# Where the steps of the adaLN product stand: eight of them from RG-LRU to the first FFN, all sixteen in pairs

## The chip, the cores and the metric

One NeuronCore of a Trainium2 chip runs the whole model as one program, written with explicit semaphores. The metric is device time of that core in microseconds. The engines are TensorE (PE), VectorE (DVE), ScalarE (ACT), GpSimd (POOL) and SyncE (SP), whose queue starts nearly all transfers of weights.

## The reference

Two blocks on a sequence of 256 tokens with 1024 features, all in float32. What matters here:

```
# first block: layer 0 = pool and attention mixer, conv FFN; layer 1 = RG-LRU mixer, conv FFN
z = causal_dwconv(h @ w_in, conv_w, conv_b)           # conv FFN, w_in 1024 x 5632
u, g = jnp.split(z, 2, axis=-1);  y = (gelu(g) * u) @ w_out
...
z = h @ w_in;  gate, xr = jnp.split(z, 2, axis=-1)    # RG-LRU, w_in 1024 x 2560
xr = causal_dwconv(xr, conv_w, conv_b)
r = sigmoid(xb @ w_a + b_a);  i = sigmoid(xb @ w_x + b_x)   # 10 blocks of 128
log_a = -8 * r * softplus(-lam);  a = exp(log_a)
b = sqrt(-expm1(2 * log_a)) * (i * xr)
hs = scan(a, b);  y = (gelu(gate) * hs) @ w_out
# second block, adaLN: needs only c, an input
mod = silu(c) @ ada_w + ada_b                          # 1024 by 1024 x 6144
sh1, sc1, gt1, sh2, sc2, gt2 = split(mod, 6)
h = rms_norm(x) * (1 + sc1) + sh1                      # first use of mod
```

## The kernel before

Activations lie transposed, features on partitions: a tile is 128 features by 256 tokens. Weights come in pieces of 128 by 8 tiles of 128 (512 KB) into a ring of nine buffers, `ring`, in the order that `weight_order` writes; piece n goes into buffer n mod 9, and SP starts its transfer once piece n - 9 has been used (`used`). ScalarE copies each piece rounded to the matmul's format (`whi`, seven buffers) and VectorE makes the rest (`wlo`); both do so in `feed`, which runs ahead of the piece at hand by a fixed number of positions in that order (ACT up to 6, DVE up to 5). A column of output, 128 features, is then 24 matmuls on TensorE: eight times whi by hh, whi by hl and wlo by hh.

The product `silu(c) @ ada_w` is cut in 24 steps (`mod_step`). A step takes two pieces of `ada_w`, which take positions in the ring but need no whi and wlo, and on TensorE four matmuls in the source (eight in the trace), each 32 columns of the array by 512. Eight steps make one part (a third of `mod`). A part's eighth step is followed by a copy to `mrow` on ScalarE, and later by `mod_turn`, which transposes the part and adds `ada_b`. The part's PSUM bank is held from its first step to that copy. The first part is made in the attention mixer. `ADA_RG` puts the second in RG-LRU: behind x columns 5, 7 and 9 and behind gate columns 1, 3, 5, 7 and 9. `ADA_IN` puts the third in the second FFN's input, behind columns 2, 5, 8, 11, 14, 17, 19 and 21. In that input a "column" m is one column of u and one of g.

RG-LRU goes like this. TensorE makes x columns 0 to 9 (0 to 2 together, with `early`), and between them the gate products `ri` for blocks whose x column is convolved (`RI`: blocks 0 and 1 behind x column 5, 2 behind 6, 3 and 4 behind 7, 5 behind 8, 6 and 7 behind 9, 8 and 9 behind gate column 0). It then makes gate columns 0 to 9 and `rg_w_out`, which takes all eight PSUM banks. VectorE, for each x column, first feeds wlo and then does the convolution (`taps`, three instructions on `xr`); later come `decline` on `rr`, `size` (on `sc` and `xr`), `inputs`, `scan`, `times_gate` and `low_of_y`, which writes `yl`. ScalarE has the sigmoids, `bends` (tanh, `xr<-rr`), `decays` (exp, `rr<-rr`), `roots` and the gelus. `size(0)` is the first that needs `decays(0)`, and `decays(0)` stands behind gate column 1 on ScalarE. The order on every engine is the order of the code.

## Time and profile before

| what | value |
|---|---|
| median of 3 runs | 1094.45 us (1092.57 to 1095.63) |
| profiled execution, its own time | 1092.14 us |
| span in the trace | 1089.8 us |
| TensorE busy | 97% of the span |
| VectorE busy | 76% |
| ScalarE busy | 57% |
| granted TensorE clock, mean | 0.989 of full speed |

The profile is of one execution, by the hardware profiler. Starts are in us from the span's start. A busy share is an average over stages with different limits, so the stages that the change touches are read one by one: the first FFN's input runs from about 126 to 242 us, RG-LRU from about 306 to 401 us, and the second FFN's input from about 413 to 540 us. "Idle before" in a row names who released the engine.

### The profile page before, as it was taken

What the parts mean: (1) busy time and instruction counts of PE and PEld (TensorE: products, weight loads), DVE (VectorE), ACT (ScalarE), POOL (GpSimd) and SP (SyncE); (2) the same over time, 40 slices, a digit from 0 to 9 for tenths busy, and PEclk for the clock granted to TensorE, in tenths of its full rate; (3) what the DMA queues carried; (4) which work ended last, traced back from release to release, by engine and by line L of the source; (5) the groups of instructions that cost most, each with busy time, mean ns of one, the idle gap of its engine ahead of it and who ended that gap; (6) DMA issues with size and microseconds to landing.
All of it is one profiled execution on the core that took longest, in us unless ns stands there. A gap on an engine that the chain in (4) does not pass through costs nothing.

```text
span 1089.8 us, 20955 instructions
## 1 busy us (share of the span) xinstructions
PE 1052.1 (97%) x8608; PEld 998.0 (92%) x8608; DVE 829.6 (76%) x1418; ACT 626.0 (57%) x1056; POOL 72.2 (7%) x79
## 2 busy tenths in 40 slices
PE   8999999999999999999999997999999999999996
PEld 7876999999998799999999897899989989999996
DVE  6466799888887979988788789998955777655452
ACT  7545686666667867665656683122343468875340
POOL 1222200000102010000001000000000030000010
PEclk8999999999999999999999999999999989999998
DMA  9358465566676956677766542232433555566651
GB/s 347 129 188 308 163 212 194 194 180 196 198 251 219 319 171 217 217 253 231 252 203 205 185 131 75 82 98 92 149 111 110 176 189 177 182 190 182 187 155 39
DMA packets 59422, 200.39 MB, mean 184 GB/s; under 512 B 6720, under 2 KB 10432, under 8 KB 59200
## 3 DMA queue, kind: packets, MB, share of 16 engines
q1 hardware_dynamic: 57600, 194.54, 55.1%
q10 hardware_dynamic: 1728, 4.53, 1.2%
q8 instruction: 68, 1.11, 0.4%
q14 instruction: 26, 0.21, 0.1%
HBM read 197.99 MB, written 1.05 MB: 183 GB/s over the span
## 4 chain that ended last, share of the span: by engine, by line
PE 83%; DVE 9%; ACT 5%; DMA 2%; issue 1%; ACTq 0%; SPq 0%; POOL 0%; DVEq 0%
PE ps L481 82%; DVE wlo L1575 2%; ACT whi L1051 1%; ACT L1051 1%; DVE rst L1608 1%; DVE raw L1575 1%; DVE hl L1575 1%; ACT raw L1051 1%; ACT hh L1051 1%; DMA ring<-rg_w_in 1%; DMA ring<-pa_w_in 0%; DMA ring<-w_o 0%; DVE bks L1575 0%; DMA ring<-pa_w_out 0%; PE ps L666 0%
## 5 line engine op out<-in xcount | busy, mean ns | idle before, releaser
L481 PE MATMUL ps<-hh,whi 128*128 128x256 f32 (+1 forms) x1656 | 473.0, 286 | 4.2 <-DVE wlo L1575 3.6
L481 PE MATMUL ps<-hl,whi 128*128 128x256 f32 (+1 forms) x1656 | 462.8, 279 | 0.0
L481 PE MATMUL ps<-hh,wlo 128*128 128x256 f32 (+1 forms) x1656 | 462.6, 279 | 0.0
L1575 DVE TENSOR_TENSOR wlo<-ring,whi 128x1024 fp32r<-128x1024 f32 (+2 forms) x314 | 376.5, 1214 | 53.0 <-ACT whi L1051 52.6
L1051 ACT ACTIVATE whi<-ring 128x1024 fp32r<-128x1024 f32 (+2 forms) x314 | 320.9, 1038 | 57.1 <-PE ps L481 39.7
L481 PEld LDWEIGHTS ps<-hh,whi 128*128 128x128 f32 x1656 | 314.8, 190 | 25.2 <-issue 14.8
L481 PEld LDWEIGHTS ps<-hl,whi 128*128 128x128 f32 x1656 | 313.3, 189 | 1.3 <-issue 1.0
L481 PEld LDWEIGHTS ps<-hh,wlo 128*128 128x128 f32 x1656 | 313.7, 189 | 0.0
L481 PE MATMUL ps<-hidh,whi 128*128 128x256 f32 x608 | 169.3, 278 | 0.0
L481 PE MATMUL ps<-hidl,whi 128*128 128x256 f32 x608 | 169.1, 278 | 0.0
L481 PE MATMUL ps<-hidh,wlo 128*128 128x256 f32 x608 | 169.1, 278 | 0.0
L481 PEld LDWEIGHTS ps<-hidh,whi 128*128 128x128 f32 x608 | 115.2, 190 | 0.8 <-issue 0.8
L481 PEld LDWEIGHTS ps<-hidl,whi 128*128 128x128 f32 x608 | 114.1, 188 | 0.0
L481 PEld LDWEIGHTS ps<-hidh,wlo 128*128 128x128 f32 x608 | 114.1, 188 | 0.0
L2380 POOL TENSOR_TENSOR sqa<-sqa,sqt 128x256 f32<-128x256 f32 x36 | 40.5, 1124 | 890.7 <-ACT sqt L1051 890.7
L1051 ACT ACTIVATE sqt<-x 128x256 f32<-128x256 f32 x49 | 20.1, 414 | 59.2 <-DVE x L1581 35.1
L1581 DVE SCALAR_TENSOR_TENSOR zg<-ps,vec,zg 128x255 f32<-128x255 f32 x84 | 40.4, 481 | 15.1 <-ACT zg L1051 11.6
L1581 DVE SCALAR_TENSOR_TENSOR zu<-ps,vec,zu 128x255 f32<-128x255 f32 x80 | 38.5, 481 | 10.4 <-ACT zu L1051 9.0
L1051 ACT ACTIVATE zg<-ps,vec 128x256 f32<-128x256 f32 x42 | 23.6, 561 | 34.0 <-PE ps L481 34.0
L1051 ACT ACT_TABLE_LOAD x32 | 41.1, 1283 | 3.3 <-PE ps L481 1.6
L481 PE MATMUL ps<-yin,ring 128*128 128x256 f32 x160 | 39.0, 379 | 0.1
L1581 DVE SCALAR_TENSOR_TENSOR x<-ps,mod,x 128x256 f32<-128x256 f32 x16 | 7.6, 483 | 40.6 <-PE ps L481 40.6
(365 smaller groups left out, 1335.3 us busy)
## 6 DMA issues: line engine op xcount, KB each, us to landing
ring<-ffn_w_in SPq DMA_DIRECT2D x88, 512.0 KB, 3.7
ring<-ffn_w SPq DMA_DIRECT2D x64, 512.0 KB, 3.9
ring<-w_in SPq DMA_DIRECT2D x51, 512.0 KB, 3.3
ring<-ada_w SPq DMA_DIRECT2D x48, 512.0 KB, 4.3
ring<-ffn_w_out SPq DMA_DIRECT2D x32, 448.0 KB, 3.4
ring<-rg_w_in SPq DMA_DIRECT2D x20, 512.0 KB, 4.6
ring<-ffn_w_out SPq DMA_DIRECT2D x16, 512.0 KB, 3.6
ring<-pa_w_in SPq DMA_DIRECT2D x15, 512.0 KB, 6.9
```

The source lines that it names most:

```text
L481: return e.matmul(o, l, r, start=start, stop=stop)
L1051: return e.activation(o, i, func, bias=bias, scale=scale, accum_out=acc)
L1575: return e.tensor_tensor(o, a, b, op)
L1581: return e.scalar_tensor_tensor(out=o, in0=a, scalar=s, in1=b, op0=op0, op1=op1)
L1608: e.reciprocal(rst[:, :], rst[:, :]).then_inc(*mean.up(("rst", n)))
L2380: e.tensor_tensor(sqa[:, :], sqa[:, :], sqt[:, m % 2, :], ADD).then_inc(*sum_g.up((n, m)))
```

## The change

The second part's eight steps are made in the first FFN's input and no longer in RG-LRU. In both FFN inputs the eight steps stand in pairs, two behind each of columns 5, 10, 15 and 20. `mod_turn` of the second part moves from the second FFN's input (column 4 on TensorE, 6 on VectorE) to the first FFN's output, where the call in `also` was there already. The number of steps, their matmuls and their transfers stay as they are. The order of the ring's pieces follows.

```
-ADA_IN = ((), (2, 5, 8, 11, 14, 17, 19, 21))
-ADA_RG = ((5, 7, 9), (1, 3, 5, 7, 9))
+ADA_IN = ((5, 5, 10, 10, 15, 15, 20, 20), (5, 5, 10, 10, 15, 15, 20, 20))
...
@@ weight_order, and in the same way conv_ffn of TensorE, VectorE and ScalarE (mod_step) @@
-            if m in ADA_IN[l]:
+            for _ in range(ADA_IN[l].count(m)):
                 columns()
...
                     whole("rg_w_in", 8, (m + 10 - 10 * n,))
-                    if m in ADA_RG[n]:
-                        columns()
...
@@ conv_ffn of TensorE; on VectorE the same with m == 6 @@
-                    if m == 4:
-                        mod_turn()
...
@@ rglru of TensorE, and in the same way of ScalarE and VectorE @@
-                    if m in ADA_RG[0]:
-                        mod_step()
...
-                    if m in ADA_RG[1]:
-                        mod_step()
```

TensorE, first FFN's input, where the g column of column 5 ends and the u column of 6 begins. Before:

```order
L481 MATMUL ps<-hh,whi_8 128x256
L481 MATMUL ps<-hl,whi_8 128x256
L481 MATMUL ps<-hh,wlo_30 128x256
L481 MATMUL ps<-hh,whi_9 128x256
L481 MATMUL ps<-hl,whi_9 128x256
L481 MATMUL ps<-hh,wlo_31 128x256
```

Now the same place reads as follows (`sc` is silu(c), and an adaLN step is two of these rows):

```order
L478 MATMUL ps<-hh,whi_8 128x256
L478 MATMUL ps<-hl,whi_8 128x256
L478 MATMUL ps<-hh,wlo_30 128x256
L478 MATMUL ps<-ring_22,sc_44 32x512 x2
L478 MATMUL ps<-ring_23,sc_44 32x512 x2
L478 MATMUL ps<-ring_15,sc_44 32x512 x2
L478 MATMUL ps<-ring_16,sc_44 32x512 x2
L478 MATMUL ps<-hh,whi_9 128x256
L478 MATMUL ps<-hl,whi_9 128x256
```

Two steps now stand where one column followed the other.

VectorE in RG-LRU, from behind the convolutions of x columns 0 to 2, which read `xl`. Before (`wlo` is a piece's low part; each group of three rows on `xr` is the taps of one column, here 3, 4 and 5):

```order
L1575 TENSOR_TENSOR wlo_32<-ring_23,whi_8 128x1024
L1581 SCALAR_TENSOR_TENSOR xr<-ps,vec,xr 128x255
L1581 SCALAR_TENSOR_TENSOR xr<-ps,vec,xr 128x254
L1581 SCALAR_TENSOR_TENSOR xr<-ps,vec,xr 128x253
L1575 TENSOR_TENSOR wlo_24<-ring_15,whi_9 128x1024
L1581 SCALAR_TENSOR_TENSOR xr<-ps,vec,xr 128x255
L1581 SCALAR_TENSOR_TENSOR xr<-ps,vec,xr 128x254
L1581 SCALAR_TENSOR_TENSOR xr<-ps,vec,xr 128x253
L1581 SCALAR_TENSOR_TENSOR xr<-ps,vec,xr 128x255
L1581 SCALAR_TENSOR_TENSOR xr<-ps,vec,xr 128x254
L1581 SCALAR_TENSOR_TENSOR xr<-ps,vec,xr 128x253
```

Now:

```order
L1562 TENSOR_TENSOR wlo_28<-ring_19,whi_8 128x1024
L1562 TENSOR_TENSOR wlo_29<-ring_20,whi_9 128x1024
L1562 TENSOR_TENSOR wlo_30<-ring_21,whi_10 128x1024
L1568 SCALAR_TENSOR_TENSOR xr<-ps,vec,xr 128x255
L1568 SCALAR_TENSOR_TENSOR xr<-ps,vec,xr 128x254
L1568 SCALAR_TENSOR_TENSOR xr<-ps,vec,xr 128x253
L1562 TENSOR_TENSOR wlo_31<-ring_22,whi_11 128x1024
L1568 SCALAR_TENSOR_TENSOR xr<-ps,vec,xr 128x255
L1568 SCALAR_TENSOR_TENSOR xr<-ps,vec,xr 128x254
L1568 SCALAR_TENSOR_TENSOR xr<-ps,vec,xr 128x253
L1562 TENSOR_TENSOR wlo_32<-ring_23,whi_12 128x1024
```

Three low parts (x columns 6, 7 and 8) stand ahead of the taps of column 3, where one stood, because no ada_w pieces take positions of the ring between them.

ScalarE in RG-LRU, from gate column 1 to `decays` (`gate<-ps` is the gate column, `xr<-rr` tanh, `rr<-rr` exp). Before:

```order
L1051 ACTIVATE gate<-ps 128x256
L1051 ACTIVATE whi_9<-ring_21 128x1024
L1051 ACTIVATE whi_10<-ring_22 128x1024
L1051 ACTIVATE xr<-rr 128x512
L1051 ACT_TABLE_LOAD
L1051 ACTIVATE rr<-rr 128x1024 x2
```

Now, with the last feed ahead of the column:

```order
L1042 ACTIVATE whi_12<-ring_21 128x1024
L1042 ACTIVATE gate<-ps 128x256
L1042 ACTIVATE xr<-rr 128x512
L1042 ACT_TABLE_LOAD
L1042 ACTIVATE rr<-rr 128x1024 x2
```

The two whi copies that stood between the gate column and tanh are gone from there; one stands ahead of the column.

## Rows read from the trace of the kernel before

**Rows 1.** The page, part 1: busy time of each engine.
```profile
PE 1052.1 (97%) x8608; PEld 998.0 (92%) x8608; DVE 829.6 (76%) x1418; ACT 626.0 (57%) x1056; POOL 72.2 (7%) x79
```

**Rows 2.** Who waited for whom, TensorE: total, times, longest.
```profile
PE ps L481 <- ACT mrow L1051: 2.6, 1, 2.6
```

**Rows 3.** Windows: busy us by engine, then TensorE's granted clock.
```profile
150.00:170.00 20.00, 20.00 (x179) 20.00 (x178) 19.68 (x35) 14.13 (x24) 0.00 (x0) 1.00 0.59 188
...
310.00:330.00 20.00, 20.00 (x156) 18.45 (x155) 19.35 (x36) 13.45 (x25) 3.16 (x3) 1.00 0.72 239
330.00:350.00 20.00, 20.00 (x147) 16.17 (x146) 14.14 (x27) 14.38 (x26) 5.34 (x7) 1.00 0.68 214
...
370.00:390.00 20.00, 17.41 (x153) 16.41 (x152) 20.00 (x27) 13.79 (x18) 0.00 (x0) 1.00 0.77 263
```

**Rows 4.** Timeline of TensorE, steps behind gate columns 1 and 3.
```profile
348.59 1.06 PE L481 MATMUL ps<-ring,sc 128*32 128x512 f32 x8
349.58 0.38 PE L481 MATMUL ps<-hh,whi 128*128 128x256 f32 x1
...
355.24 1.07 PE L481 MATMUL ps<-ring,sc 128*32 128x512 f32 x8
```

**Rows 5.** Timeline of TensorE, second half of that first step.
```profile
349.04 0.61 PE L481 MATMUL ps<-ring,sc 128*32 128x512 f32 x4
```

**Rows 6.** TensorE, steps of the second FFN: first pair of rows.
```profile
444.42 1.07 PE L481 MATMUL ps<-ring,sc 128*32 128x512 f32 x8
...
461.95 1.06 PE L481 MATMUL ps<-ring,sc 128*32 128x512 f32 x8
```

**Rows 7.** TensorE, steps of the second FFN: second pair of rows.
```profile
514.53 1.06 PE L481 MATMUL ps<-ring,sc 128*32 128x512 f32 x8
...
526.61 1.07 PE L481 MATMUL ps<-ring,sc 128*32 128x512 f32 x8
```

**Rows 8.** TensorE in RG-LRU: x column 6, then gate products.
```profile
322.39 0.38 PE L481 MATMUL ps<-hh,whi 128*128 128x256 f32 x1
...
328.93 1.89 PE L481 MATMUL ps<-xr,wab 128*128 128x256 f32 x8
```

**Rows 9.** TensorE in RG-LRU: gate products of blocks 8 and 9.
```profile
343.94 1.89 PE L481 MATMUL ps<-xr,wab 128*128 128x256 f32 x8
```

**Rows 10.** VectorE in RG-LRU.
```profile
320.39 1.23 DVE L1575 TENSOR_TENSOR wlo<-ring,whi 128x1024 fp32r<-128x1024 f32 x1
...
339.15 1.52 DVE L1581 SCALAR_TENSOR_TENSOR xr<-ps,vec,xr 128x255 f32<-128x255 f32 x3 [0.25 <-ACT xr L1051]
...
353.90 1.23 DVE L1575 TENSOR_TENSOR sc<-rr 128x1024 f32<-128x1024 f32 x1 [1.48 <-ACT rr L1051]
...
366.07 1.23 DVE L1575 TENSOR_TENSOR wlo<-ring,whi 128x1024 fp32r<-128x1024 f32 x1 [1.05 <-ACT whi L1051]
...
377.06 0.68 DVE L1575 TENSOR_TENSOR yl<-gate,yh 128x512 fp32r<-128x512 f32 x1
```

**Rows 11.** ScalarE in RG-LRU.
```profile
348.70 0.38 ACT L1051 ACTIVATE gate<-ps 128x256 f32<-128x256 f32 x1 [1.04 <-PE ps L481]
348.98 2.00 ACT L1051 ACTIVATE whi<-ring 128x1024 fp32r<-128x1024 f32 x2
350.88 0.62 ACT L1051 ACTIVATE xr<-rr 128x512 f32<-128x512 f32 x1
```

**Rows 12.** TensorE at the start of rg_w_out.
```profile
378.83 0.36 PE L481 MATMUL ps<-yh,whi 128*128 128x256 f32 x1 [2.59 <-ACT mrow L1051]
```

**Rows 13.** Landing times of ada_w pieces.
```profile
DMA to landing us min/median/max: 3.6/4.3/8.2
```

**Rows 14.** TensorE in the mixers behind its longest wait.
```profile
672.63 1.12 PE L481 MATMUL ps<-ws,gvT 128*64 128x128 f32 x16 [3.40 <-ACT gvT L1051]
```

**Rows 15.** Windows behind that wait: busy us, TensorE's granted clock.
```profile
672.00:676.00 4.00, 3.37 (x28) 3.23 (x29) 3.89 (x8) 2.95 (x6) 0.00 (x0) 0.75 0.02 4
676.00:680.00 4.00, 3.94 (x24) 3.37 (x25) 3.83 (x18) 2.66 (x4) 0.00 (x0) 0.82 0.11 33
```

More of the change, by code:

```diff
@@ L709, in conv_ffn @@
                     give((w, m + 22), ff_dve, (l, "g", m))
-                    if m in ADA_IN[l]:
+                    for _ in range(ADA_IN[l].count(m)):
                         mod_step()
-                    if m == 4:
-                        mod_turn()
                 def also(m):
@@ L1272, in conv_ffn @@
                     behind(m)
-                    if m in ADA_IN[l]:
+                    for _ in range(ADA_IN[l].count(m)):
                         mod_step()
@@ L1338, in rglru @@
                         ri(i)
-                    if m in ADA_RG[0]:
-                        mod_step()
                 bends(0)
@@ L1347, in rglru @@
                         act(gate[:, m, :], out_of("rg_w_in", m), ACT.Gelu_apprx_tanh).then_inc(*rg_act.up(("gelu", m)))
-                    if m in ADA_RG[1]:
-                        mod_step()
                     for i in RI[m + 10]:
@@ L1924, in conv_ffn @@
                     behind(m)
-                    if m in ADA_IN[l]:
+                    for _ in range(ADA_IN[l].count(m)):
                         mod_step()
-                    if m == 6:
-                        mod_turn()
                 behind(22)
@@ L2000, in rglru @@
                         decline(i)
-                    if m in ADA_RG[0]:
-                        mod_step()
                 for m in range(10):
@@ L2006, in rglru @@
                         decline(i)
-                    if m in ADA_RG[1] and m < 9:
-                        mod_step()
                     for g in {2: (0, 1), 3: (2,)}.get(m, ()):
@@ L2021, in rglru @@
                         low_of_y(2)
-                        mod_step()
                 for k in range(10):
```

## The prediction

> **What bounds the kernel now.** I read the busy times first. TensorE works for 1052.1 us [rows 1] of a span of 1089.8, so only some 38 us of the span are waits, and a change that moves TensorE's work can win or lose only what waits before or after it. The list of who waited for whom shows where: of the waits in the stages that the change touches only one is of any size, 2.6 us put down to ScalarE's `mrow` copy [rows 2]. It stands at the start of `rg_w_out`, at 378.83 [rows 12]. The windows by stage then say what is behind it. In the first FFN's input TensorE is busy for 20.00 of 20 us while VectorE is at 19.68 (150 to 170). In RG-LRU TensorE is also at 20.00 until 370, with VectorE at 19.35 from 310 to 330 and at 14.14 from 330 to 350; from 370 to 390 TensorE falls to 17.41 and VectorE has 20.00 [rows 3]. So the first FFN's input is bound by TensorE alone, whatever VectorE's load. RG-LRU begins bound by TensorE with VectorE nearly full, and ends on a chain through VectorE. That is the point of the whole forecast: work taken off TensorE in RG-LRU comes back only as far as VectorE and ScalarE get done earlier, while the same work put in the FFN costs its full length.
>
> **What a step costs.** Between the starts of two steps of RG-LRU lie 6.65 us, which hold one step and two columns (348.59 and 355.24) [rows 4]. In the second FFN 17.53 us hold one step and six columns [rows 6] and 12.08 us hold one step and four [rows 7]. The difference of the last two gives a column 5.45 / 2 = 2.725 us, and what is left is 1.18 us for a step there; in RG-LRU it is 6.65 - 5.45 = 1.20. I take 1.20.
>
> **What a second step behind the first costs.** The trace of before has no such pair. A step is eight matmuls, four at a time on four strips of the array. Its first four start at 348.59, its second four at 349.04 [rows 5], and the next column's first matmul at 349.58 [rows 4]. Four thus follow four at 0.45 us, and going back to whole-array matmuls takes 0.54; the rest of the 1.20 is going in and loading weights. A second step should add 2 x 0.45 = 0.90, so a pair costs 2.10 where two single steps cost 2.40. Bounds: no gain, 0, if each step pays its entry again, and 0.30 a pair if not. I take 0.30, because the four second matmuls of a step already follow its first four without a gap for the change of pieces (they read the step's second half).
>
> The Trainium skill, on TensorEngine Tiling (Array Packing), Key Properties, says that changing the tiling mode drains the array; by it a pair pays that once for two steps, and the sum would be the same as mine.
>
> **The sum, part by part.** First FFN's input: eight steps come in, as four pairs, 4 x 2.10 = +8.4. Nothing hides them, since TensorE has no idle time there [rows 3]. Second FFN's input: eight single steps become four pairs, 4 x (2.10 - 2.40) = -1.2. `mod_turn` of the second part (a copy's transposes, in any place on TensorE) only moves from one stage bound by TensorE to another, and I cost it at nothing.
>
> RG-LRU: eight steps go, 9.6 us of TensorE's work. How much earlier does `rg_w_out` start? I follow the chain.
>
> 1. VectorE up to the taps of x column 9. They end at 339.15 + 1.52 = 340.67 [rows 10]. From 320.39 it is nearly full. Without ada_w pieces in the ring its feed runs farther ahead, and nine low parts, not six, stand ahead of those taps. Three more at some 1.15 us end the taps 3.45 us later, less the idle time that they fill. The work from 320.39 counts to 22.6 us at the pace of its own rows (9 low parts at 1.15, 7 taps at 1.52, 1.6 of `decline`), so the taps end between 343.0 and 343.9 us. I take 343.4.
> 2. TensorE wants those taps for the gate products of block 9. Without steps it starts x column 6 when its low part is made, 320.39 + 1.15 = 321.55, where it started at 322.39 [rows 8, 10]. From there to the products of blocks 3 and 4 are 6.54 us (322.39 to 328.93) [rows 8], and from those to block 8's product 15.01 us (to 343.94) [rows 9], of which 2.40 were the steps behind x columns 7 and 9. Block 8's product now starts at about 321.55 + 6.54 + 12.61 = 340.7, and block 9's could at 341.65. It waits until 343.4. From products of both blocks to the end of gate column 1 were 343.94 to 348.59 [rows 4, 9], 4.65; less 0.95 for block 8 that is 3.7. Gate column 1 ends at 347.1, 1.5 earlier than before, not the 3.6 of the three steps that went.
> 3. ScalarE. Behind gate column 1 it made two high parts for 1.90 us (348.98 to 350.88), then tanh, a table load and exp, and VectorE began `size` at 353.90 [rows 10, 11]. Now both high parts are gone from there. `size` starts 1.5 + 1.9 = 3.4 earlier, at 350.5.
> 4. VectorE from `size` to the first `yl`: 353.90 to 377.06 + 0.68 = 377.74, of which it idled 1.05 [rows 10]. The chain has six low parts before and after, so its work is the same 22.8 us, and the low parts' high parts are ready earlier. That is 1.05 more, and the first `yl` is done at 373.3.
> 5. `rg_w_out` began 1.09 behind that `yl`, since it takes all eight banks and one was freed only by `mrow` [rows 2, 12]. No part is held in RG-LRU now: 1.0 more.
>
> Together 1.5 + 1.9 + 1.05 + 1.0 = 5.5 us earlier. TensorE itself would be there at 347.1 + 8 x 2.725 = 368.9, so it waits 4.4 us where it waited 2.59: what is late next is `yl`. Bounds of the 5.5: 9.6 if TensorE alone decided (plus the old wait of 2.59 at most); below, 4.0, if point 1 costs all that the three steps gave and only points 3 to 5 stay.
>
> Sum: 8.4 - 1.2 - 5.5 = +1.7 us. On the profiled execution that is 1092.14 + 1.7 = 1093.8. The median of the runs lies 2.3 above that execution, so for a median I say 1096.1.
>
> **The rivals.** (a) RG-LRU gives everything back. For it speaks that VectorE had 5.9 idle us from 330 to 350 [rows 3]; against it that the idle time stands behind the stretch where it is full. Then the sum is 8.4 - 1.2 - 9.6 = -2.4, and with the old wait gone too -5.0. Chance 0.12.
>
> (b) The pairs hold TensorE up in the FFNs. Four pieces of a nine-deep ring are then ada_w's. Behind column 5 the piece of u column 8 starts its transfer only when g column 5 is used; ScalarE stands in its queue waiting for it ahead of the last tap of u column 6, and VectorE behind ScalarE. TensorE wants u column 8 only 2.1 + 4 x 2.725 = 13.0 us later, and a landing takes 4.3, at most 8.2 us [rows 13], plus 2.2 for the parts. It would decide from a landing of 10.8 us on; each us beyond costs up to 8 for eight pairs, +9.7 with the 1.7. Chance 0.08.
>
> (c) The longer wait lowers TensorE's clock. Behind a wait of 3.40 us [rows 14] the granted clock was 0.75 and then 0.82 in two stretches of 4 us [rows 15], a loss of 1.00 + 0.72 = 1.7 us; around the present wait of 2.59 it stayed at 1.00 [rows 3]. A wait of 4.4 us is beyond both. The same loss again makes +3.4. Against it: whether a wait of that length hits is not decided by its length alone, as far as two cases can show. Chance 0.25.
>
> The Trainium skill, on TensorE: Matmul & The Clock Gate, HAM oscillation, warns that a longer gap of idle time throttles the array to half its clock and that the matmuls behind it start cold. By that rule (c) would be the rule and not a rival, and the change would come out at +3.4.
>
> (d) Something else, mostly VectorE later than in point 1, as the feed order changes in three stages: 0.05.
>
> **How the numbers follow.** My forecast, +1.7, has 0.50. About 0.3%, 3.3 us, is what a measurement of this kernel can tell from no change. From the forecast's own bounds (RG-LRU 4.0 to 7.5, pairs 0 to 2.4) its range is -0.3 to +5.6, and some 0.08 of its 0.50 lie above 3.3; of (c) half does, (b) and (d) all; of (a) 0.05 is beyond -3.3. That gives faster 0.06, same 0.64, slower 0.30. The range takes in (a) without its end, and (c) with the forecast's worse half: from -4.5 to +5.5 on 1094.45 with the spread of medians, 1090.5 to 1100.
>
> **What would show it.** In the changed profile: pairs of 16 small matmuls of about 1.95 us; no wait on TensorE in either FFN's input; the first FFN's input longer by 8.4 us and the second's shorter by 1.2; in RG-LRU a wait of about 1 us ahead of block 9's product for VectorE's taps; the first `size` 3.4 us earlier relative to the stage; a wait near 4.4 us at `rg_w_out` for `yl`, with the granted clock there saying whether (c) holds. I am wrong if VectorE's early low parts do not delay the taps, or if TensorE waits in the FFNs.

## The result and the profile after

The changed kernel takes 1104.63 us (median of 12 runs, 1096.47 to 1108.92). Beside it the kernel before took 1091.74 us (12 runs, 1083.15 to 1099.54). The ratio of the two, made from runs side by side, is 1.0104, with a 95% interval of 1.0077 to 1.0131: 11.4 us slower (8.4 to 14.3), where the sum had +1.7. So the change is slower by more than can be put down to chance, and the time lies outside the range.

The profiled execution of the changed kernel took 1100.17 us. The page's first part, to be laid beside [rows 1]:

```profile
span 1097.7 us, 20957 instructions
PE 1054.6 (96%) x8608; PEld 1002.1 (91%) x8608; DVE 832.7 (76%) x1418; ACT 625.3 (57%) x1056; POOL 73.6 (7%) x79
```

TensorE does the same 8608 matmuls and is busy 2.5 us longer. Who waited for whom on TensorE (total, times, longest), the counterpart of [rows 2]:

```profile
PE ps L478 <- DVE wlo L1562: 6.4, 9, 1.6
PE ps L478 <- ACT gate L1042: 4.9, 1, 4.9
...
PE ps L478 <- DVE xr L1568: 2.3, 2, 1.2
```

The wait for `mrow` is gone. In its place stands one of 4.9 us put down to `gate`, and two for the taps (`xr`). These are small numbers beside 11.4, so I went to the ends of the stages. They can be read off TensorE's timeline: the two-matmul row sum that opens each stage, and the first product with `hidh`, which opens an FFN's output. Before, and then after:

```profile
122.52 0.59 PE L481 MATMUL ps<-sqa,cst 128*128 128x256 f32 x2
...
241.99 0.28 PE L481 MATMUL ps<-hidh,whi 128*128 128x256 f32 x1
...
303.87 0.59 PE L481 MATMUL ps<-sqa,cst 128*128 128x256 f32 x2
...
410.09 0.67 PE L481 MATMUL ps<-sqa,cst 128*128 128x256 f32 x2 [1.76 <-POOL sqa L2380]
...
539.70 0.39 PE L481 MATMUL ps<-hidh,whi 128*128 128x256 f32 x1
```

```profile
118.94 0.59 PE L478 MATMUL ps<-sqa,cst 128*128 128x256 f32 x2
...
248.56 0.28 PE L478 MATMUL ps<-hidh,whi 128*128 128x256 f32 x1
...
311.41 0.59 PE L478 MATMUL ps<-sqa,cst 128*128 128x256 f32 x2
...
417.12 0.67 PE L478 MATMUL ps<-sqa,cst 128*128 128x256 f32 x2 [1.77 <-POOL sqa L2360]
...
547.69 0.28 PE L478 MATMUL ps<-hidh,whi 128*128 128x256 f32 x1
```

What stands ahead of the first of these rows is the same work in both kernels, and its length differs from execution to execution (118.9 to 124.9 us in my profiles). The spans of two profiles therefore say less than the stages. Each kernel was profiled a second time. All lengths are in us, each the difference of two such rows:

| stage | before | before, 2nd | after | after, 2nd |
|---|---|---|---|---|
| first FFN, input | 119.47 | 119.46 | 129.62 | 129.84 |
| first FFN, output | 61.88 | 61.89 | 62.85 | 62.86 |
| RG-LRU up to `rg_w_out` | 74.96 | 74.82 | 71.95 | 71.62 |
| `rg_w_out` to the next row sum | 31.26 | 32.12 | 33.76 | 33.55 |
| second FFN, input | 129.61 | 129.20 | 130.57 | 130.55 |
| second FFN, output | 62.59 | 62.59 | 62.76 | 63.68 |

Against the sum: the first FFN's input lost 10.2, not 8.4; RG-LRU gave 3.0 to 3.2, not 5.5; behind it 1.4 to 2.5 us are lost; the second FFN's input is 1.0 to 1.4 us longer, where 1.2 less was forecast.

**What happens in the first FFN.** The pair costs what was forecast. A pair and the matmuls on either side:

```profile
180.59 0.28 PE L478 MATMUL ps<-hh,whi 128*128 128x256 f32 x1
...
180.93 0.28 PE L478 MATMUL ps<-hh,whi 128*128 128x256 f32 x1
...
181.15 0.28 PE L478 MATMUL ps<-hh,wlo 128*128 128x256 f32 x1
181.36 1.92 PE L478 MATMUL ps<-ring,sc 128*32 128x512 f32 x16
183.21 0.38 PE L478 MATMUL ps<-hh,whi 128*128 128x256 f32 x1
...
184.14 0.28 PE L478 MATMUL ps<-hl,whi 128*128 128x256 f32 x1
...
184.49 0.28 PE L478 MATMUL ps<-hl,whi 128*128 128x256 f32 x1
```

The last full matmul starts at 181.15 and the next at 183.21: 2.06 us. The same two starts around a single step lie 1.20 us apart in the kernel before. But look at the starts on either side. Ahead of the pair, 180.59 to 180.93, three matmuls take 0.34; behind it, 184.14 to 184.49, three take 0.35. Over longer stretches it is 113.3 ns a matmul ahead and 118 ns behind. A column of 24 is then 2.72 or 2.83 us. Windows of 20 us without a step show it in the count of matmuls (the first number in brackets), at a TensorE that is busy throughout and a granted clock of 1.00:

```profile
155.00:175.00 20.00, 20.00 (x179) 20.00 (x178) 18.09 (x29) 11.77 (x20) 0.00 (x0) 1.00 0.80 270
185.00:205.00 20.00, 20.00 (x173) 20.00 (x172) 17.44 (x28) 11.49 (x19) 0.00 (x0) 1.00 0.77 263
215.00:235.00 20.00, 20.00 (x179) 20.00 (x178) 17.74 (x29) 11.49 (x19) 0.00 (x0) 1.00 0.81 268
```

So there are two **cadences**, and no view calls either one idle time. In the changed kernel every pair turns the one into the other: slow up to the pair at 152, fast to 181, slow to 212, fast to 241, slow behind, and likewise in the second FFN (451, 480, 511, 540). Before, this stage was slow up to about 144 and fast from there to its end, with 179 matmuls in 150 to 170 [rows 3].

**What happens in the second FFN.** Besides the cadence there is a wait. It stands ahead of u column 3; the row of the changed kernel, then the same matmul before, where it follows the step behind column 2 without a wait:

```profile
434.09 0.36 PE L478 MATMUL ps<-hh,whi 128*128 128x256 f32 x1 [1.57 <-DVE wlo L1562]
```

```profile
427.05 0.36 PE L481 MATMUL ps<-hh,whi 128*128 128x256 f32 x1
```

Counted from the stage's row sum the two starts are the same, 16.97 and 16.96 us. In all 15 profiles of this case, eight with a step behind column 2 and seven without one, it is 16.95 to 16.97. So VectorE's low part sets when u column 3 starts, and the step that stood behind column 2 filled time in which TensorE would have waited.

**What happens in RG-LRU.** TensorE's waits there, then VectorE's rows around them:

```profile
338.70 0.38 PE L478 MATMUL ps<-hh,whi 128*128 128x256 f32 x1 [1.07 <-DVE xr L1568]
...
351.94 1.10 PE L478 MATMUL ps<-xr,wab 128*128 128x256 f32 x4 [1.21 <-DVE xr L1568]
...
383.36 0.55 PE L478 MATMUL ps<-yh,whi 128*128 128x256 f32 x1 [4.88 <-ACT gate L1042]
```

```profile
327.92 3.50 DVE L1562 TENSOR_TENSOR wlo<-ring,whi 128x1024 fp32r<-128x1024 f32 x3
...
350.29 1.50 DVE L1568 SCALAR_TENSOR_TENSOR xr<-ps,vec,xr 128x255 f32<-128x255 f32 x3
...
360.18 1.23 DVE L1562 TENSOR_TENSOR sc<-rr 128x1024 f32<-128x1024 f32 x1 [1.94 <-ACT rr L1042]
...
382.17 0.68 DVE L1562 TENSOR_TENSOR yl<-gate,yh 128x512 fp32r<-128x512 f32 x1
```

The three low parts at 327.92 are those of the order listing. The wait at 338.70 ends when the taps of x column 5 do (337.14 + 1.50 = 338.64): x column 8 takes the PSUM bank that x column 5 had, and VectorE's taps have to read it first. Then the granted clock (the number behind the fifth pair of brackets) behind the wait of 4.88 us:

```profile
384.00:388.00 4.00, 4.00 (x21) 4.00 (x21) 4.00 (x7) 2.24 (x4) 0.00 (x0) 0.50 0.00 0
388.00:392.00 4.00, 4.00 (x34) 4.00 (x34) 4.00 (x6) 1.90 (x3) 0.00 (x0) 0.91 0.44 131
```

It is 0.50 and then 0.91: rival (c) has come true.

### The profile page after: what moved, and what is told of

Same layout as the page of the kernel before. It is cut to its first block, busy times and chain, and to the rows that moved or that the text cites. A ratio compares the mean times of both kernels' runs of the same rounds, so it can differ in the third digit from the quotient of the medians.

```text
span 1097.7 us, 20957 instructions
## 1 busy us (share of the span) xinstructions
PE 1054.6 (96%) x8608; PEld 1002.1 (91%) x8608; DVE 832.7 (76%) x1418; ACT 625.3 (57%) x1056; POOL 73.6 (7%) x79
## 3 DMA queue, kind: packets, MB, share of 16 engines
HBM read 197.99 MB, written 1.05 MB: 181 GB/s over the span
## 4 chain that ended last, share of the span: by engine, by line
PE 69%; DVE 20%; ACT 7%; issue 2%; DMA 2%; ACTq 0%; SPq 0%; DVEq 0%
PE ps L478 68%; DVE wlo L1562 6%; ACT whi L1042 2%; DVE xr L1568 2%; ACT L1042 1%; DVE hl L1562 1%; ACT hh L1042 1%; DVE rst L1595 1%; DVE raw L1568 1%; DVE raw L1562 1%; DMA ring<-ffn_w_out 1%; ACT raw L1042 1%; DVE x L1562 1%; DMA ring<-pa_w_in 1%; DMA ring<-w_o 0%
## 5 line engine op out<-in xcount | busy, mean ns | idle before, releaser
L1042 ACT ACTIVATE zu<-ps,vec 128x256 f32<-128x256 f32 x40 | 22.4, 561 | 40.5 <-DVE hidl L1562 28.4
```

The costliest lines, as they stand in the source:

```text
L1042: return e.activation(o, i, func, bias=bias, scale=scale, accum_out=acc)
```

## The experiments

Three theories stood at the start. **T1**: the pairs as such cost time in the FFNs. **T2**: low parts made too early in RG-LRU delay the taps. **T3**: the wait at `rg_w_out` drops the clock. The second round asked what turns the cadence. All ratios are to the kernel before in the same series. In e6, e7, c1 and d1 matmuls or transposes are added whose result nothing reads.

**e1_single: the changed kernel with single steps.**

```
-ADA_IN = ((5, 5, 10, 10, 15, 15, 20, 20), (5, 5, 10, 10, 15, 15, 20, 20))
+ADA_IN = ((2, 5, 8, 11, 14, 17, 19, 21), (2, 5, 8, 11, 14, 17, 19, 21))
```

> As the changed kernel, but the steps in both FFNs' inputs stand singly, behind columns 2, 5, 8, 11, 14, 17, 19 and 21. The traces before and after show TensorE's matmuls of a column start every 113.3 ns in some stretches and every 118 ns in others, at full clock, and in the changed kernel the two alternate at every pair of steps (118 until the pair behind column 5, 113 until the one behind 10, 118, 113, 118), 0.11 us per column. Theory A (a pair turns one cadence into the other, a single step doesn't): the move alone costs 9.6 - 3.0 (what RG-LRU gave back in the trace) and up to 2.5 for the clock at rg_w_out, so +6.5 to +9 us against the kernel before, and each FFN's input keeps one cadence from end to end. Theory B (the pairs themselves are what made it slow, the move is nearly free): 0 to +2 us. Theory C (cadence is unrelated to the steps): alternations at the same columns as in the changed kernel.

Measured: 1101.89 us (7 runs), ratio 1.0098 (1.0052 to 1.0143). The first FFN's input took 132.56 us, slow cadence from end to end. The second took 132.69, slow too from u column 3 on, though its single steps are those of before (129.61). So single steps don't cure the loss; T1 isn't its main cause. What e1 and before differ in there is `mod_turn`, which no longer stands behind column 4.

**e2_pairs: the kernel before with pairs in the second FFN.**

```
-ADA_IN = ((), (2, 5, 8, 11, 14, 17, 19, 21))
+ADA_IN = ((), (5, 5, 10, 10, 15, 15, 20, 20))
...
-            if m in ADA_IN[l]:
+            for _ in range(ADA_IN[l].count(m)):
```

> The kernel before with the steps of the second FFN's input in pairs behind columns 5, 10, 15 and 20; RG-LRU keeps its eight. Theory A: four pairs are 1.2 us shorter than eight single steps (the changed kernel's trace shows 1.92 us for 16 small matmuls), and the cadence alternates in that FFN only, so about half of its 40 columns are slow: +2.2 us if the stretch was fast before, 0 on average if it was not; together -1 to +1. Theory B: the pairs carry half of the loss, +4 to +6 us.

Measured: 1094.73 us (12 runs), ratio 1.0045 (1.0008 to 1.0081), slower. The stages ahead of it are as before; the second FFN's input took 132.15 us for 129.61, although four pairs are 1.4 us shorter than eight single steps. The cadence turned at each pair here too. But cadence is not all of it: without the step behind column 2 u column 3 starts no earlier (a wait of 1.54 us stands there, at 427.33), and TensorE waited another 0.67 us for VectorE's `mod` at 458.80.

**e3_threes: the changed kernel with groups of three.**

```
-ADA_IN = ((5, 5, 10, 10, 15, 15, 20, 20), (5, 5, 10, 10, 15, 15, 20, 20))
+ADA_IN = ((4, 4, 4, 12, 12, 12, 20, 20), (4, 4, 4, 12, 12, 12, 20, 20))
```

> As the changed kernel, but with three steps behind column 4, three behind 12 and two behind 20 in both FFNs' inputs. Theory A in the form that an even number of steps turns the cadence and an odd one doesn't: one cadence from the start to column 20. Theory A in the form that anything longer than a single step turns it: it turns at 4, 12 and 20. Time against the kernel before: +5 to +9 by the move (9.6 less about 3 that the groups save, less 3.0 from RG-LRU, plus up to 2.5 for the clock), and 0 to +4 of cadence on top.

Measured: 1107.58 us (6 runs), ratio 1.0143 (1.0096 to 1.0191). Its four groups of three kept the cadence they met, two fast and two slow; its two pairs turned it. Each group of three is followed by a wait for VectorE's low part, 0.94 us, 3.8 us in all, which no pair has. So rival (b) of the prediction is right for three steps in a row:

```profile
451.11 0.36 PE L478 MATMUL ps<-hh,whi 128*128 128x256 f32 x1 [0.94 <-DVE wlo L1562]
```

**e4_lag: e1 with VectorE's feed held back two pieces in RG-LRU.**

```
                 for m in range(3, 10):
-                    feed(tail("rg_w_in", m + 10))
+                    feed(tail("rg_w_in", m + 10) - 2)
...
-                    feed(tail("rg_w_in", m))
+                    feed(tail("rg_w_in", m) - (2 if m < 2 else 0))
```

> As e1_single, but in RG-LRU VectorE feeds the low parts two positions later, up to gate column 1, so that seven and not nine stand ahead of the taps of x column 9. Theory A says that the low parts made early delay the taps (3.6 us in the changed kernel's trace, where TensorE waited 1.07 us for block 4's and 1.21 us for block 9's): without that TensorE doesn't wait for taps, and rg_w_out starts some 2.5 us earlier than in e1_single, unless the low parts come late instead. Rival: ScalarE's or VectorE's total work in the stage sets the start of rg_w_out whatever the order, and then it starts within 0.5 us of e1_single.

Measured: 1101.67 us (11 runs), ratio 1.0070 (1.0036 to 1.0103). Up to `rg_w_out` RG-LRU took 69.47 us for e1's 71.84. TensorE's waits in the stage, all of them:

```profile
332.52 0.38 PE L478 MATMUL ps<-hh,whi 128*128 128x256 f32 x1 [0.19 <-DVE wlo L1562]
...
384.21 0.55 PE L478 MATMUL ps<-yh,whi 128*128 128x256 f32 x1 [4.87 <-ACT gate L1042]
```

Both waits for taps are gone (in e1 they were 1.07 and 1.02 us). T2 is shown: with the same steps, only the place of the low parts gives 2.4 us. The wait of 4.87 stays, because TensorE comes earlier as well.

**e5_turn4: e1 with `mod_turn` back behind column 4 of the second FFN.**

```
+                    if m == 4:
+                        mod_turn()
 
                 def also(m):
-                    mod_turn()
+                    if l:
+                        mod_turn()
```

> As e1_single, but the second part's four transposes stand behind column 4 of the second FFN's input again, where the kernel before had them, and not in the first FFN's output. In all traces so far the matmuls behind those transposes start every 113.3 ns until the next wait; in the kernel before they turned the second FFN's input from 118 to 113.3 at column 4 (129.61 us for the stage), in e1_single that stage kept 118 (132.69 us). Theory D (the transposes set the faster cadence): the second FFN's input takes 129.6 us again, and the first FFN's output keeps the cadence of its input, so it is 62 us less 0.5 for the transposes if that input was fast and 2 us longer if slow; the total is 1 to 4 us below e1_single. Rival (the cadence changes at chance places): 129.6 or 132.7 whatever the transposes.

Measured: 1104.59 us (11 runs), ratio 1.0084 (1.0049 to 1.0118). The second FFN's input took 129.22 us for e1's 132.69. The same window in e1 and in e5:

```profile
500.00:520.00 20.00, 20.00 (x170) 19.03 (x169) 15.55 (x27) 12.66 (x22) 0.00 (x0) 1.00 0.71 235
```

```profile
500.00:520.00 20.00, 20.00 (x176) 19.04 (x175) 16.06 (x28) 13.03 (x23) 0.00 (x0) 1.00 0.79 260
```

170 matmuls became 176. But the transposes didn't do that in this profile. The columns ahead of the transposes, which stand at 451.83, ran at 113.3 ns already from about 446 on, where e1's at the same place ran at 118; so that e5 came out as expected is luck. That the transposes can do it is seen where the stage was slow ahead of them: in before (117.8 ns up to 438.43, 113.3 behind), e2 (438.71) and c2 (452.09). c2 has the same single steps as e1 in this stage and the same wait of 0.57 us, and takes 129.61 us for e1's 132.69. So taking the transposes out costs 3.1 us where the stage starts slow, and nothing where it starts fast. The median doesn't show it: the intervals of e1 and e5 are wider than that, and against e1's profile e5's lost 1.7 us in the first FFN's output, which has no transposes now, 2.3 in the mixers and 6.3 in the last FFN, where the code is e1's (175.44 and 181.73).

**e6_fill: the changed kernel with eight matmuls ahead of `rg_w_out`.**

```
+                p = take("fill")
+                for _ in range(8):
+                    f = mm(p[:, 0:T], ones, C("iota"))
+                f.then_inc(*rg_pe.up("fill"))
+                give("fill", rg_pe, "fill")
                 outs = [take(("rg_w_out", m)) for m in range(8)]
```

> The changed kernel with eight matmuls of constants (128x128 by 128x256, their result unused) between the last gate column and rg_w_out, some 3.6 us of the 4.9 us that TensorE waits there. All four profiles of kernels without steps in RG-LRU show the granted clock at half for 6.8 us right behind that wait, and 33.5 to 33.9 us from the start of rg_w_out to the next row sum, against 31.3 in the kernel before. Theory (the wait lowers the clock): that stretch takes 31.3 us again, 2.3 us less in all than the changed kernel, if the fillers don't outlast the wait. Rival (the clock falls for another reason): no change of the stretch, and the fillers cost nothing or up to 1 us.

Measured: 1102.97 us (12 runs), ratio 1.0077 (1.0047 to 1.0108). The timeline's wait, and the windows behind it:

```profile
384.22 0.36 PE L478 MATMUL ps<-yh,whi 128*128 128x256 f32 x1 [2.58 <-DVE xr L1969]
```

```profile
384.00:388.00 4.00, 3.78 (x32) 3.81 (x33) 4.00 (x7) 1.57 (x3) 0.00 (x0) 1.00 0.00 0
388.00:392.00 4.00, 4.00 (x36) 4.00 (x36) 4.00 (x6) 3.18 (x4) 0.00 (x0) 1.00 0.61 182
```

The clock stays at 1.00, and the stretch behind takes 32.13 us for 33.76. T3 is shown for this place: the eight matmuls fill part of the wait, and behind the 2.58 us that are left the clock stays up (c1, with 1.52 us left, agrees). The gain in the median, 0.3%, is within the intervals.

**e7_turns: the kernel before with four transposes of a constant in two places** (behind column 4 of the first FFN's input, and behind column 5 of `ffn_w1`, the last FFN).

```
+            def spare(n):
+                p = take(("spare", n))
+                for q in range(4):
+                    f = e.transpose(p[:, q * 128:q * 128 + 128], blk, ident)
+                f.then_inc(*ada_pe.up(("spare", n)))
+                give(("spare", n), ada_pe, ("spare", n))
```

> The kernel before with four more transposes of constants (result unused, some 0.5 us) behind column 4 of the first FFN's input and behind column 5 of the last FFN's. Theory D: both stages run at 113.3 ns per matmul behind them whatever they ran at before; the last FFN takes 176 us, where it took 181.7 in four of six profiles and 175.4 in two, so 0 to 6 us less than the kernel before, 3 to 4 in the median, and the runs spread less. Rival: the last FFN's 181.7 or 175.4 comes by chance and the medians agree within 1.5 us, 1 us slower for the transposes.

Measured: 1093.04 us (12 runs), ratio 1.0003 (0.997 to 1.0037). Neither place turned the cadence: the first FFN's input met it slow and stayed slow (123.95 us), and so did the last FFN (182.16). Its first FFN:

```profile
150.00:290.00 140.00, 140.00 (x1191) 140.00 (x1190) 122.62 (x242) 88.95 (x146) 2.94 (x4) 1.00 0.60 182
```

Up to column 4 this is the code of before, whose two profiles were fast there. So the cadence in which a stretch starts is not set by its own code.

**e8_odd: the kernel before, second FFN with two groups of three and two singles.**

```
-ADA_IN = ((), (2, 5, 8, 11, 14, 17, 19, 21))
+ADA_IN = ((), (5, 5, 5, 12, 12, 12, 17, 20))
```

> The kernel before with the second FFN's eight steps as three behind column 5, three behind 12 and one each behind 17 and 20. Like e2_pairs it saves re-entries: 4 x 1.20 + 4 x 0.83 = 8.1 us against 9.6. Theory A (an even number of steps turns the cadence, an odd one doesn't): the whole stage behind column 4 stays at 113.3 ns, it takes 128.1 us (e2_pairs 132.15, before 129.61), and the kernel is 1.5 us faster than before in the median. Rival (any group turns it): 130 to 132 us.

Measured: 1101.73 us (12 runs), ratio 1.0060 (1.0025 to 1.0094). The second FFN's input took 133.20 us. Between the two groups of three and behind the second:

```profile
460.00:480.00 20.00, 19.68 (x167) 19.48 (x167) 18.97 (x31) 15.55 (x25) 0.00 (x0) 1.00 0.74 263
...
510.00:530.00 20.00, 20.00 (x176) 19.03 (x175) 18.53 (x36) 13.62 (x24) 0.00 (x0) 1.00 0.65 205
```

The cadence turned at both groups, where in e3 four groups of three had not turned it. The guess that an even number of steps turns and an odd one doesn't has fallen. Of the 133.20 us, 3.2 are waits that the expectation didn't have: 1.03 ahead of u column 3, 0.94 behind each group and 0.32 for `mod`.

**c1_mended: the changed kernel with the lag of e4, the fill of e6 and four transposes of `mrow` behind column 4 of the second FFN.**

```
+                    f = e.transpose(p[:, q * 128:q * 128 + 128], mrow[:, q * 128:q * 128 + 128], ident)
...
+                    if l and m == 4:
+                        again()
```

> The changed kernel with three mends: VectorE's feed in RG-LRU two positions later up to gate column 1 (as e4_lag), the eight filling matmuls ahead of rg_w_out (as e6_fill), and four transposes of mrow, result unused, behind column 4 of the second FFN's input. If the losses are the ones read so far, they add up: 2.4 us from the feed, 1.6 to 2.5 from the clock, and about half of the second FFN's input at the faster cadence as before. Against the changed kernel 4 to 6 us less, against the kernel before +0.4 to +0.6%. What stays is 8.1 us of pairs in the first FFN against some 5.5 that RG-LRU gives back. Rival (something else in the move costs the time): +0.8% or more remains. For the cadence: if transposes of mrow turn it where e7_turns' transposes of constants didn't, the columns between column 4 and the first pair run at 113.3 ns.

Measured: 1100.83 us (12 runs), ratio 1.0094 (1.0061 to 1.0127). The mends do what they should each in its stage: RG-LRU 69.59 us, the stretch behind it 31.26. But the first FFN's input is 129.85, and the second's 131.24: its pairs undo behind column 5 what the transposes set behind column 4, and the wait ahead of u column 3 stays (1.56 us). The median is worse than expected. By the expectation's own mark, +0.8% or more, its rival holds and something else costs time too; but 4 us less than the changed kernel would also lie within the two intervals.

**c2_early8: the kernel before with the eighth step of RG-LRU behind gate column 7, so that the `mrow` copy is early.**

```
-ADA_RG = ((5, 7, 9), (1, 3, 5, 7, 9))
+ADA_RG = ((5, 7, 9), (1, 2, 3, 5, 7))
```

> The kernel before with the second part's eight steps in RG-LRU behind x columns 5, 7, 9 and gate columns 1, 2, 3, 5, 7, so that the part's bank is copied out a column and a half ahead of rg_w_out. In the kernel before rg_w_out began 1.09 us behind the first yl, for the mrow copy. Expected: rg_w_out starts 0.6 to 1.1 us earlier (74.96 us from the row sum in the kernel before, now 73.9 to 74.4), no wait on mrow, total the same as before within what the runs tell. Rival: the step behind gate column 2 makes VectorE's chain late instead and the stage is as long as before or longer.

Measured: 1098.86 us (12 runs), ratio 1.0082 (1.0049 to 1.0115). RG-LRU up to `rg_w_out` took 79.65 us for 74.96, with this wait:

```profile
389.38 0.55 PE L481 MATMUL ps<-yh,whi 128*128 128x256 f32 x1 [6.37 <-ACT gate L1051]
```

The clock fell behind it too, and the stretch behind took 34.36 us. `rg_w_out` begins 0.5 us behind the first `yl` here, where it was 1.09, so the early `mrow` gives 0.6. But that `yl` is done 5.3 us later than before. `size` starts 2.1 us later, and behind it ScalarE waits 3.30 us for a transfer of gate weights (`ring<-rg_w_in`, at 365.82) where it waited 1.05 before. The rival was right.

**c3_before and c4_after** are the second profiles in the table above.

> The kernel before, once more, for a second profile of the same code. If the cadence of a stage comes by chance in each execution, some stage is at another cadence than in the first profile: the first FFN's input 123.7 where it was 119.47 us, or the last FFN 175.4 where it was 181.72. If it belongs to the code, all stages agree within 0.3 us.

> The changed kernel, once more. The clock falls again behind the wait at rg_w_out (33.5 to 33.9 us from there to the next row sum). Both FFNs' inputs alternate again at the pairs; whether they begin fast or slow may differ, and the stage takes 129.6 or 130 us either way since half of it is at each cadence.

Measured: 1090.11 and 1105.3 us. The stages of the FFNs and of RG-LRU agree with the first profiles within 0.4 us, but for the stretch behind `rg_w_out` in the kernel before (32.12 for 31.26, slow from its start) and the second FFN's output in the changed one (63.68 for 62.76, with a wait of 0.38 us). The changed kernel's clock fell again. Its pairs turned the cadence again too, but in the first FFN the other way round: that input now began fast, so that it is slow behind the first pair and fast behind the second, at the same length of 129.8 us:

```profile
160.00:180.00 20.00, 20.00 (x172) 20.00 (x172) 17.44 (x29) 11.48 (x19) 0.00 (x0) 1.00 0.76 266
190.00:210.00 20.00, 20.00 (x179) 20.00 (x178) 17.24 (x28) 11.69 (x20) 0.00 (x0) 1.00 0.79 270
```

So one and the same code meets either cadence.

**d1_mrow: e7 with one word changed, its transposes read `mrow`.**

```
-                    f = e.transpose(p[:, q * 128:q * 128 + 128], blk, ident)
+                    f = e.transpose(p[:, q * 128:q * 128 + 128], mrow[:, q * 128:q * 128 + 128], ident)
```

> As e7_turns (the kernel before with four more transposes behind column 4 of the first FFN's input and behind column 5 of the last FFN's, result unused), but they read mrow, as the kernel's own do, and not a constant. In 13 of 13 places so far the matmuls behind the kernel's own transposes of mrow run at 113.3 ns, whatever they ran at before; behind e7_turns' transposes of a constant they stayed at 118 ns, twice of twice. If what is read decides: the first FFN's input takes 120.0 us and the last FFN 175.9 in the profile, and the kernel is 3 to 6 us faster than before. If the place in the program or chance decides: 118 ns stays in one of the two at least, and the total agrees with the kernel before within what the runs tell.

Measured: 1088.09 us (12 runs, 1084.23 to 1094.56) for 1093.01 of before (17 runs), ratio 0.9969 (0.994 to 0.9999), the one version below both kernels, though only just clear of no change. The last FFN took 176.00 us for 181.72. Its transposes, and the last FFN's window, in d1; then the same window in e7 (before has 1021):

```profile
915.09 0.60 PE L591 MATMUL ps<-cst,mrow 128*128 128x128 f32 x4
```

```profile
950.00:1070.00 120.00, 120.00 (x1061) 120.00 (x1060) 58.53 (x64) 58.71 (x91) 6.74 (x6) 1.00 0.54 166
```

```profile
950.00:1070.00 120.00, 120.00 (x1022) 120.00 (x1021) 61.57 (x67) 63.02 (x100) 6.00 (x5) 1.00 0.58 176
```

1061 matmuls stand where 1021 or 1022 stood. Four transposes of 0.6 us shorten a stage of 182 us by 5.7. In the first FFN of this profile the cadence was fast already ahead of the transposes, so that place tells nothing. What sets transposes of `mrow` apart from those of a constant rests on this one place against e7's two.

Two things in d1's profile go against what was believed so far. The single step behind column 2 of the second FFN turned the cadence. And the clock fell in `rg_w_out` behind a wait of only 1.95 us. The windows on either side of that step, and the one of the clock:

```profile
415.00:425.00 10.00, 10.00 (x88) 10.00 (x87) 9.88 (x25) 5.48 (x12) 0.00 (x0) 1.00 0.51 170
428.00:438.00 10.00, 10.00 (x91) 10.00 (x90) 9.71 (x16) 8.28 (x15) 0.00 (x0) 1.00 0.82 290
```

```profile
380.00:384.00 4.00, 4.00 (x27) 4.00 (x26) 4.00 (x6) 1.94 (x3) 0.00 (x0) 0.68 0.49 176
```

## Why the prediction was wrong

Four terms of the sum +1.7 were off. The second FFN's input was put at -1.2 and grew by 1.2. RG-LRU was put at -5.5 and gave 3.0, because step 2 of its chain failed. The clock's fall was left to a rival and costs 2.0. And the cost of a column was taken as fixed where it has two values.

**What bounds the kernel: right, but read too coarsely.** The first FFN's input is bound by TensorE alone, before and after, and so is the second's but for its start, up to u column 3. But "bound by TensorE" was taken to mean a fixed time per column. I had 2.725 us a column from [rows 6] and [rows 7], and that was the fast cadence. The slow one, 2.83, is in the trace of before as well: its last FFN has 1021 matmuls in 120 us, 117.5 ns each, against the 179 of 20 us in [rows 3]. I had not compared stages.

**First FFN's input, +8.4: the term is right, the stage is not.** A pair costs 2.03 us by the stage's length and 2.06 by the starts around it, for the 2.10 forecast; four are 8.1 to 8.2. The pair saves 0.34 to 0.37 over two single steps at 1.20, where I had 0.30. The stage lost 10.2 in the profiles; the 2.1 more is cadence. The kernel before has this stage at either cadence: 119.5 fast (twice before, and e2) and 123.5 slow (e8 and c2, the same code up to there). The changed kernel alternates, so it has the mean of both in every execution: (119.5 + 123.5) / 2 + 8.1 = 129.6, and 129.6 to 129.9 was measured four times (after twice, e6, c1). Against a before of both kinds in equal parts the loss is the 8.1 of the steps.

**Second FFN's input, -1.2: this step failed.** It consists of two sentences of the prediction: that four pairs save 1.2, and that `mod_turn` "only moves", costed at nothing. The pairs save 1.4 by their own length (4 x 0.34), and the transposes take 0.5 with them. But the stage grew by 1.0 to 1.4 us, so 2.8 to 3.2 came on top. It has two parts.

- 1.2 us are a saving that could not be had. The step behind column 2 was one of the eight that I took away at 1.20 each, and it had cost nothing: u column 3 starts 16.96 us behind the row sum with it and 16.97 without it. Four pairs stand against seven steps that counted, 8.2 us against 8.4.
- The other 1.6 to 2.0 are cadence. Before, `mod_turn` behind column 4 puts the stage on the fast cadence in every profile or finds it there (129.2 to 129.6 in before, its second profile, e5, e7, c2 and d1; 132.7 without it in e1 and e4). Now it is slow from u column 3 on, and the pairs turn it to and fro.

An edit that I had costed at nothing is worth 3.1 us with single steps and a slow start, as c2 against e1 shows. In e2 the transposes are there and the pairs alone lose part of the fast stretch.

**RG-LRU, -5.5: half of it came.** Step by step, in times from the stage's row sum:

- Step 1, the taps of x column 9 end at 40.4 (350.29 + 1.50 - 311.41), where the kernel before had 36.8 [rows 10]: 3.6 later and not 2.7. The cause was right, and e4 shows it. A first price of it was missed: the same three low parts also hold up the taps of x column 5, whose PSUM bank x column 8 needs, and TensorE waited 1.07 us for them, at 338.70. (The expectation of e4 put this wait down to block 4; but block 3's and 4's products had run by then, from 335.74.) The second wait, forecast as about 1 us, was 1.21.
- Step 2 is the one that failed. Gate column 1 should have ended 1.5 earlier. ScalarE copied it 0.7 us later than before: 356.89 - 311.41 = 45.5, against 348.70 - 303.87 = 44.8 [rows 11]. Both waits for taps stand ahead of it. And ScalarE's row shows a link that I had left out:

```profile
354.98 1.06 ACT L1042 ACTIVATE xr<-rr 128x1024 f32<-128x1024 f32 x1 [1.06 <-DVE rr L1565]
355.95 1.04 ACT L1042 ACTIVATE whi<-ring 128x1024 fp32r<-128x1024 f32 x1
356.89 0.37 ACT L1042 ACTIVATE gate<-ps 128x256 f32<-128x256 f32 x1
357.15 0.62 ACT L1042 ACTIVATE xr<-rr 128x512 f32<-128x512 f32 x1
```

  The tanh of the second group waits for VectorE's `decline` of block 7, and the high part and the gate column stand in its queue. So the delay of VectorE reaches `decays` by a second way.
- Step 3, `size` starts 1.3 us earlier (48.8 for 50.0), not 3.4: the 1.9 of the two high parts was right, the 1.5 was -0.7.
- Step 4, the first `yl` is done 2.4 us earlier (71.4 for 73.9), so 1.1 us more than `size`, as forecast (1.05).
- Step 5 gives 0.6 and not 1.0: `rg_w_out` begins 0.51 behind the first `yl`, where it was 1.09. Together 3.0 in the first profiles and 3.2 in the second. The wait there is 4.88 us, forecast 4.4.

**The rivals.** (a), that RG-LRU gives everything back, didn't happen. (b), that the pairs hold TensorE up, didn't either: no pair of the changed kernel has a wait behind it. A wait in an FFN was named as a sign of being wrong, though, and the one ahead of u column 3 is there, for another reason than (b)'s. (c) happened: the clock fell at the wait in all six profiles that have no steps in RG-LRU and no fill (after, its second, e1, e3, e4, e5; waits of 4.9 to 5.9 us) and in c2's, with 6.37. The granted 0.50 is the lower of the clock's two levels, 1.2 GHz. Of the eight profiles with a wait of 1.46 to 2.59 us seven kept the clock at 1.00, e6 and c1 among them; d1 with its 1.95 didn't. So the fall came behind each of the seven long waits and behind one of the eight short ones; the length alone doesn't decide, as (c) had said.

The fall costs some 2.0 us (33.65 us for the stretch, mean of two profiles, for 31.7), near the 1.7 I gave it. With a full clock the stretch takes 31.3 or 32.1 us, by cadence, and with the fall 32.7 to 34.4. Only the chance of (c), 0.25, was too low. The Trainium skill had said so (TensorE: Matmul & The Clock Gate, HAM oscillation: a longer gap drops the clock), and the trace agrees, with 0.50 granted behind 4.88 us; d1's fall behind 1.95 us is beyond what that section says.

The prediction's last figures have two slips, which change nothing above: its own terms for slower add up to 0.34 (0.08 + 0.125 + 0.08 + 0.05), not 0.30, and 1094.45 - 4.5 is 1090.0, not 1090.5.

**The new sum.** With the first FFN's input at +8.1, its output at -0.3 (the code of before has 61.9 or 64.3, after has 62.9), RG-LRU at -2.9, the stretch behind it at +2.0, the second FFN's input at +1.2 and its output at up to +1, I come to about +9. Measured are +11.4, 8.4 to 14.3. The sum lies in the interval, and some 2.4 us of the middle value are not attributed. Each of its terms rests on two to four profiles, in a kernel whose runs spread by 1.5%; and c1, whose three mends should have won 5 us, is hardly faster in its ratio. Perhaps the cadence of the mixers and the last FFN, which differs between executions, hides it; no run here shows that. This stays open.

## What to carry to other kernels

Before you cost a stage that is bound by TensorE, take the spacing of its matmuls from that stage itself, in several stages and more than one execution, and ask for each edit in it, a few transposes too, whether the spacing behind it is still the one ahead. Before you credit a step that goes, look whether the next instruction starts earlier without it, or only waits. Where a queue loses work, its neighbours run farther ahead: list what moves in front of the instruction for which the critical engine waits, and follow each of its readers and not only the last. Work that moves out of a stage may leave a wait long enough for the clock to fall; price that as the likely case when the trace already shows the fall behind a shorter one.

## What the runs showed of the hardware

**Two cadences at one clock.** Back-to-back 128 by 256 matmuls, each with its own weights, start every 113.3 ns or every 118 ns, at a granted clock of 1.00 both times and with TensorE busy at 100%. The Trainium skill gives the time from start to start of back-to-back matmuls as the columns over 2.4 GHz plus about 2.5 ns (TensorE: Matmul & The Clock Gate, "Wait — 56ns, not 53.3ns?"). For 256 columns that makes an estimate of 109.2 ns; both spacings measured here are longer, and 113.3 is the nearer. In a stage of 44 columns the difference is 4 us (119.5 or 123.5), in the last FFN 6.3 (175.4 or 181.7).

What changes it, as far as counted in the 15 profiles:

- Behind the groups of four transposes of `mrow` it was fast in all 48 places, though slow ahead in 19 of them. Transposes of a constant left it slow (2 of 2).
- Pairs of steps turned it in all 38 places (after, its second, e6, c1, e2, and e3's pairs behind column 20).
- Groups of three turned it in e8 (2 of 2) and not in e3 (4 of 4).
- Single steps kept it in nearly all places, but not always. Behind gate column 1 in RG-LRU a single step turned slow into fast in four profiles (117.9 to 113.3 ns; before at 348.59, its second, e2, d1) and left it slow in e7, e8 and c2; and there is d1's in the second FFN.
- The first columns of a stage are slow in some and fast in others: in the second FFN of the changed kernel they run at 113.4 ns from 417.9 to 432.2, in the kernel before at 117.8 from 410.8 to 425.8.

Behind a wait it may start in either, with the same code: the first FFN's input was fast from about 144 us on in before, its second profile and e2 and d1, and slow in e7, e8 and c2. What it is physically no run here tells. Nor does any run show a rule that gives all of these places. That stays open.

**It explains part of the spread.** Runs of the kernel before go from 1081 to 1101 us. One FFN's input at the other cadence is 4 us and the last FFN 6, so several such chances add up to a spread of that size; that it is all of it was only argued.
